# The compression MLP's first product in true fp32 on four column tiles, from raw weights in idle buffers

## The reference, cut to what matters

```python
blk_idx = arange(15)[:, None] * 16 + arange(32)[None, :]       # 15 blocks of 32 tokens, stride 16
def compress(x, w1, w2, pe):                                     # x: (B, 256, 2 heads, 128)
    xb = x[:, blk_idx] + pe[None, None, :, None, :]
    xb = moveaxis(xb, 3, 2).reshape(B, 15, 2, 32 * 128)
    return gelu(xb @ w1) @ w2                                    # w1: (4096, 128), w2: (128, 128)
kc = compress(k_cmp, cmp_w1[0], cmp_w2[0], cmp_pe[0])
vc = compress(v_cmp, cmp_w1[1], cmp_w2[1], cmp_pe[1])
```

## Time and profile before

| | |
|---|---|
| median of 3 runs | 1335.93 us |
| span of the profiled execution | 1336.1 us |
| PE (matmul) busy | 1319.3 us, 99% |
| PEld (weight load) busy | 967.8 us, 72% |
| DVE busy | 581.0 us, 43% |
| ACT busy | 487.0 us, 36% |
| POOL busy | 28.6 us, 2% |
| DMA | 364.96 MB, mean 273 GB/s |

### The profile page before, as it was taken

One profiled execution on the slowest core, in us unless ns is written; L12 is line 12 of the kernel. 1 busy time (PEld: TensorE's weight loads), 2 busy tenths in 40 slices (PEclk: granted clock), 3 DMA queues, 4 the chain that ended last, 5 costly groups with the idle time before them and its releaser, 6 DMA issues.

```text
span 1336.1 us, 17829 instructions
## 1 busy us (share of the span) xinstructions
PE 1319.3 (99%) x7317; PEld 967.8 (72%) x7317; DVE 581.0 (43%) x752; ACT 487.0 (36%) x678; POOL 28.6 (2%) x50
## 2 busy tenths in 40 slices
PE   8999999999999999999999999999999999999898
PEld 8999989998888888888888888854444444534343
DVE  4387444446555545554445555525111121121206
ACT  4454444435465644454333434422121221211212
POOL 1000000400000000000100001000000000000000
PEclk9999999999999999999999999999999999999999
DMA  9767555545545445654556795799999999999996
GB/s 304 259 196 261 178 189 189 189 159 166 173 137 179 155 149 173 192 162 163 183 198 215 265 391 187 254 383 415 422 421 420 422 421 422 421 420 422 421 408 244
DMA packets 122099, 364.96 MB, mean 273 GB/s; under 512 B 11627, under 2 KB 19243, under 8 KB 98486
## 3 DMA queue, kind: packets, MB, share of 16 engines
q1 hardware_dynamic: 115430, 359.06, 72.6%
q10 hardware_dynamic: 6608, 5.02, 1.3%
HBM read 361.96 MB, written 2.10 MB: 272 GB/s over the span
## 4 chain that ended last, share of the span: by engine, by line
PE 93%; DMA 4%; DVE 1%; SPq 1%; ACT 0%; issue 0%; DVEq 0%
PE main L1204 19%; PE main L1206 19%; PE main L1205 19%; PE main L561 16%; PE att L651 7%; PE att L515 5%; DMA mraw<-in_expert_w_down_dram 3%; PE att L1453 1%; DMA raw<-in_w_in_dram 1%; PE main L527 1%; PE main L528 1%; PE att L1436 1%; PE att L1472 1%; PE att L1468 1%; PE att L1423 0%; PE att L622 0%
## 5 line engine op out<-in xcount | busy, mean ns | idle before, releaser
L1870 DVE TENSOR_TENSOR wlo<-raw,whi 128x2048 fp32r<-128x2048 f32 x134 | 308.1, 2299 | 354.1 <-ACT whi L1619 354.1
L1619 ACT ACTIVATE whi<-raw 128x2048 fp32r<-128x2048 f32 x134 | 256.1, 1911 | 413.7 <-PE main L1206 410.7
L561 PE MATMUL main<-mraw,xg 128*64 128x512 f32 x1024 | 225.3, 595 | 0.7 <-DMA mraw<-in_expert_w_up_dram 0.6
L1204 PE MATMUL main<-whi,xhi 128*128 128x512 f32 (+1 forms) x544 | 203.8, 375 | 0.0
L1206 PE MATMUL main<-whi,xlo 128*128 128x512 f32 (+1 forms) x544 | 201.7, 371 | 0.0
L1205 PE MATMUL main<-wlo,xhi 128*128 128x512 f32 (+1 forms) x544 | 201.5, 370 | 0.0
L561 PEld LDWEIGHTS main<-mraw,xg 128*64 128x64 f32 x1024 | 71.9, 137 | 136.9 <-issue 134.9
L1204 PE MATMUL main<-xhi,whi 128*128 128x256 f32 (+1 forms) x560 | 159.5, 285 | 1.6 <-DVE wlo L2002 1.0
L1205 PE MATMUL main<-xlo,whi 128*128 128x256 f32 (+1 forms) x560 | 158.4, 283 | 0.0
L1206 PE MATMUL main<-xhi,wlo 128*128 128x256 f32 (+1 forms) x560 | 158.4, 283 | 0.0
L1206 PEld LDWEIGHTS main<-whi,xlo 128*128 128x128 f32 x544 | 102.5, 188 | 17.7
(11 more groups left out here) (345 smaller groups left out, 1353.8 us busy)
## 6 DMA issues: line engine op xcount, KB each, us to landing
raw<-in_w_in_dram SPq DMA_DIRECT2D x95, 1024.0 KB, 5.0
mraw<-in_expert_w_gate_dram SPq DMA_DIRECT2D x64, 1024.0 KB, 22.6
mraw<-in_expert_w_up_dram SPq DMA_DIRECT2D x64, 1024.0 KB, 23.7
mraw<-in_expert_w_down_dram SPq DMA_DIRECT2D x58, 1024.0 KB, 24.4
raw<-in_w_branch_dram SPq DMA_DIRECT2D x24, 1024.0 KB, 5.0
raw<-in_w_out_dram SPq DMA_DIRECT2D x16, 1024.0 KB, 6.4
mraw<-in_expert_w_down_dram SPq DMA_DIRECT2D x12, 512.0 KB, 8.2
xin<-in_x_dram SPq DMA_DIRECT2D x4, 512.0 KB, 8.1
```

The source lines that it names most:

```text
L561: ins = pe.matmul(main[0][half, w, :], xg[:, k, half], src[:, kk * DE:(kk + 1) * DE], start=(k == 0), stop=(k == KT - 1))
L1204: pe.matmul(o, ah, bh, start=start, stop=False, skip_group_check=skip)
L1619: act.activation(whi[:, u % SPLIT, 0:n], raw[:, slot, 0:n], ACT.Copy).then_inc(hi_done, 1)
L1870: dve.tensor_tensor(wlo[:, u % SPLIT, 0:n], raw[:, slot, 0:n], whi[:, u % SPLIT, 0:n].bitcast(F32), ALU.subtract).then_inc(lo_done, 1)
```

## The change

The four units of `cmp_w1` leave the ring. SyncE loads them unsplit into four buffers that nothing uses yet, each right after the ring's loads of units 9 to 12. The sum of windows and `pe` is written with a stride of 32 in place of 30, the two columns left over are set to zero by VectorE, and its high and low parts are not made. TensorE computes, for each position l, a true fp32 matmul with a stationary 128x32 and a moving 128x128, on column tile l mod 4; tile n gathers the positions with l mod 4 = n. The four partial sums lie in the four groups of 32 partitions. One fp32 matmul for each of keys and values, against `pick` (four identities of 32, made by GpSimd), adds them and transposes. All later units of the ring are four numbers lower, and the work hung on them moves with them. Some semaphores are merged.

```diff
-        w1u = len(units)
-        for j in range(2):
-            for q in range(2):
-                src = A["cmp_w1"][0, j, q * 2048:(q + 1) * 2048, :].rearrange("(l p) m -> p l m", p=P)
-                units.append((src, 16, P))
-        HALVED = [1, *range(w1u, w1u + 5)]
+        HALVED = [1]
-        xpk = at("xpk", R + 4096, [P, XP])
+        xpk, xpv = at("xpk", R + 4096, [P, CMP, CT]), at("xpv", O1, [P, CMP, CT])
+        w1 = [at(f"w1_{n}", o, [P, 16, P]) for n, o in enumerate((made["qaT"], made["qbT"], O2 + 8192, O1 + 4096))]
@@ SyncE, after load(u, ...)
+                if SLC0 <= u < SLC0 + 4:
+                    n = u - SLC0
+                    rows = A["cmp_w1"][0, n // 2, n % 2 * 2048:(n % 2 + 1) * 2048, :]
+                    sp.dma_start(w1[n][:], rows.rearrange("(l p) m -> p l m", p=P)).then_inc(w1_in[n // 2], 16)
@@ GpSimd, at the start
+            ch.link(pool.memset(pick[:], 0.0))
+            for n in range(P // CT):
+                ins = pool.affine_select(out=pick[:], in_=pick[:], compare_op=ALU.not_equal, fill=1.0, base=-CT * n,
+                                         pattern=[[-1, CT]], channel_multiplier=1)
...
@@ TensorE
-            for j, (xh, xl) in enumerate(((xpkh, xpkl), (xpvh, xpvl))):
...
-                        ins = mm3(att[0:LB * KV * NC, 3 - 2 * j, :], xh[:, cols], xl[:, cols],
...
+            for j, x_ in enumerate((xpk, xpv)):
+                pe.wait_ge(xp_sum, j + 1)
+                pe.wait_ge(w1_in[j], 32)
+                for l in range(CMP):
+                    n = l % (P // CT)
+                    ins = pe.matmul(att[n * CT:(n + 1) * CT, 3 - 2 * j, 0:P], x_[:, l, :], w1[2 * j + l // 16][:, l % 16, :],
+                                    start=(l < P // CT), stop=(l >= CMP - P // CT), skip_group_check=True)
+            ins.then_inc(xp_ps, 1)
@@ TensorE, compress2, after the first unit of win
-                        for l in range(LB):
-                            ins = pe.matmul(att[:, 3, j * 32:j * 32 + n], cs[0:LB * n, j, l * P:(l + 1) * P],
...
+                        ins = pe.matmul(att[:, 3, j * CT:(j + 1) * CT], cs[:, j, :], pick[:], start=(j == 0), stop=True,
+                                        skip_group_check=True)
@@ ScalarE, extra(u)
-                if u == 12:
-                    for j, (a, b) in enumerate(((xpk, xpkh), (xpv, xpvh))):
...
-                if u == w1u + 5:
-                    act.wait_ge(unit_used, w1u + 4)
+                if u == last("slc") + 2:
+                    act.wait_ge(xp_ps, 1)
-                if u == w1u + 7:
+                if u == last("slc") + 4:
@@ VectorE, extra(u)
                 if u == 11:
+                    for dst in (xpk, xpv):
+                        ins = dve.memset(dst[:, :, KV * NC:], 0.0)
+                    link(ins)
...
-                if u == 13:
-                    for j, (a, b, c) in enumerate(((xpk, xpkh, xpkl), (xpv, xpvh, xpvl))):
...
-                if 19 <= u < 23:
+                if 15 <= u < 19:
                     top_rounds(2)
```

More of the change, by code:

```diff
@@ L55 @@
 C_QB, C_CKV, C_QI, C_KI, C_UV, C_GM = 2584, 3608, 3864, 4120, 4188, 6236
-LB = 4
 CW, CG = 16, 32
+CT = 32
 NKI = ID + IH
@@ L197, in build @@
         kcT, vcT = at("kcT", R, [P, KV, S]), at("vcT", R + 2048, [P, KV, S])
-        XP = CMP * KV * NC
-        xpk = at("xpk", R + 4096, [P, XP])
[L200 to L204, removed]
+        xpk, xpv = at("xpk", R + 4096, [P, CMP, CT]), at("xpv", O1, [P, CMP, CT])
+        w1 = [at(f"w1_{n}", o, [P, 16, P]) for n, o in enumerate((made["qaT"], made["qbT"], O2 + 8192, O1 + 4096))]
         ws = at("ws", O1 + 12288, [P, GG, P])
@@ L221, in build @@
         smT = at("smT", made["pT"] + 7168, [P, S])
-        cs = at("cs", made["wuk"], [P, 2, LB * P])
+        cs = at("cs", made["wuk"], [P, 2, P])
+        pick = at("pick", made["wuk"] + 2048, [P, CT])
         score = at("score", made["sig"], [P, 3 * P])
@@ L319, in build @@
         part_in = [sem(f"part_in{k}") for k in range(4)]
-        gn_in, pe_in, pe_ps, pe_out, w2_in, kvg_in, late_in = sems("gn_in pe_in pe_ps pe_out w2_in kvg_in late_in")
+        gn_in, pe_in, pe_ps, pe_out, early_in, late_in = sems("gn_in pe_in pe_ps pe_out early_in late_in")
         ki_ps, ki_out, ix_ps, ix_sum, ix_mask = sems("ki_ps ki_out ix_ps ix_sum ix_mask")
         c_ssq, c_var, c_std, c_norm, c_ps, c_out = sems("c_ssq c_var c_std c_norm c_ps c_out")
-        xp_sum, xp_hi, xp_lo, cs_out, g1_ps, g1_out, cc_ps, cc_out = sems("xp_sum xp_hi xp_lo cs_out g1_ps g1_out cc_ps cc_out")
-        ws_in, ws_ps, ws_out, ws_ok, gsig = sems("ws_in ws_ps ws_out ws_ok gsig")
+        xp_sum, xp_ps, cs_out, g1_ps, g1_out, cc_ps, cc_out = sems("xp_sum xp_ps cs_out g1_ps g1_out cc_ps cc_out")
+        w1_in = [sem(f"w1_in{j}") for j in range(2)]
+        ws_ps, ws_out, ws_ok, gsig = sems("ws_ps ws_out ws_ok gsig")
         v_var, v_std, v_nrm, v_ok, mix_ps, mix_u, oc_hi = sems("v_var v_std v_nrm v_ok mix_ps mix_u oc_hi")
@@ L1034, in build @@
         block = ctx.enter_context(nc.Block())
-        N_CONST = 1 + 2 * T + HEADS + 1 + 5
+        N_CONST = 1 + 2 * T + HEADS + 1 + 5 + 1
+        SLC0 = chunks["slc"][1]
         @block.sync
@@ L1141, in _ @@
                 pool.memset(blank, 0.0).then_inc(consts, 1)
+            ch.link(pool.memset(pick[:], 0.0))
+            for n in range(P // CT):
+                ins = pool.affine_select(out=pick[:], in_=pick[:], compare_op=ALU.not_equal, fill=1.0, base=-CT * n,
+                                         pattern=[[-1, CT]], channel_multiplier=1)
+                if n < P // CT - 1:
+                    ch.link(ins)
+            ins.then_inc(consts, 1)
             pool.wait_ge(ix_sum, 1)
@@ L1366, in compress2 @@
                     pe.wait_ge(cs_out, 1)
-                    n = KV * NC
+                    pe.wait_ge(consts, N_CONST)
                     for j in range(2):
-                        for l in range(LB):
-                            ins = pe.matmul(att[:, 3, j * 32:j * 32 + n], cs[0:LB * n, j, l * P:(l + 1) * P],
-                                            ident[0:LB * n, l * n:(l + 1) * n], start=(j == 0 and l == 0),
-                                            stop=(l == LB - 1), skip_group_check=True)
+                        ins = pe.matmul(att[:, 3, j * CT:(j + 1) * CT], cs[:, j, :], pick[:], start=(j == 0), stop=True,
+                                        skip_group_check=True)
                     ins.then_inc(g1_ps, 1)
@@ L1375, in compress2 @@
                     pe.wait_ge(g1_out, 1)
-                    pe.wait_ge(w2_in, 16)
+                    pe.wait_ge(early_in, 48)
                     pe.matmul(att[:, 3, 0:KV * NC], w2[:, 0, :], g1[:], start=True, stop=True)
@@ L1381, in compress2 @@
                 if u == last("win"):
-                    pe.wait_ge(ws_in, 16)
+                    pe.wait_ge(early_in, 48)
                     for g in range(GG):
@@ L1687, in extra @@
                     act.activation(rstd[:], ssq[:], ACT.Sqrt).then_inc(c_std, 1)
-                if u == 12:
-                    for j, (a, b) in enumerate(((xpk, xpkh), (xpv, xpvh))):
-                        act.wait_ge(xp_sum, j + 1)
-                        act.activation(b[:], a[:], ACT.Copy).then_inc(xp_hi, 1)
                 if u == last("slc") + 3:
@@ L1694, in extra @@
                     act.activation(cT[:].rearrange("p c s -> p (c s)"), att[:, 2, :], ACT.Copy).then_inc(c_out, 1)
-                if u == w1u + 5:
-                    act.wait_ge(unit_used, w1u + 4)
+                if u == last("slc") + 2:
+                    act.wait_ge(xp_ps, 1)
                     for j in range(2):
-                        ins = act.activation(cs[0:LB * KV * NC, j, :], att[0:LB * KV * NC, 3 - 2 * j, :], ACT.Copy)
+                        ins = act.activation(cs[:, j, :], att[:, 3 - 2 * j, 0:P], ACT.Copy)
                     ins.then_inc(cs_out, 1)
-                if u == w1u + 7:
+                if u == last("slc") + 4:
                     act.wait_ge(g1_ps, 1)
@@ L1760, in _ @@
                 if u == 1:
-                    act.dma_start(w2[:], A["cmp_w2"][0].rearrange("a m d -> m a d")).then_inc(w2_in, 16)
-                    act.dma_start(kvg[:], A["kv_norm_g"].to_broadcast([P, LAT])).then_inc(kvg_in, 16)
-                    act.dma_start(ws[:], A["gmlp_w_s"][0].rearrange("g t s -> t g s")).then_inc(ws_in, 16)
+                    act.dma_start(w2[:], A["cmp_w2"][0].rearrange("a m d -> m a d")).then_inc(early_in, 16)
+                    act.dma_start(kvg[:], A["kv_norm_g"].to_broadcast([P, LAT])).then_inc(early_in, 16)
+                    act.dma_start(ws[:], A["gmlp_w_s"][0].rearrange("g t s -> t g s")).then_inc(early_in, 16)
                 if u in after:
@@ L1932, in extra @@
                     link(dve.reciprocal(rstd[:], rstd[:]))
-                    dve.wait_ge(kvg_in, 16)
+                    dve.wait_ge(early_in, 48)
                     for t in range(T):
@@ L1944, in extra @@
```

(10 more changed lines are left out.)

## The result

The changed kernel took 1328.62 us (median of 4 runs, 1328.30 to 1330.33) where the kernel before took 1335.88 (4 runs in all): 7.3 us faster, ratio 0.9946, interval 0.9935 to 0.9958. A repeat with more runs gave 1327.04 against 1335.71, ratio 0.9937 (0.9924 to 0.9951). The forecast was 1327.6, 8.3 us faster, with a range of 1326.8 to 1331.2.

A forecast was written before the change was run, and what follows sets the result against it. PE, busy 99% of the span, was taken to bound the kernel. Product -7.4, gathering -1.25 and VectorE +0.3 gave -8.3 us, from the median 1335.93 to 1327.6 us; whole range 1326.8 to 1331.2.

The forecast's parts named there:

- The product: First product on PE: 32 waves of four records at 0.110 us plus 0.32, so 11.26 to 3.9 us, saving 7.4.
- the edges: Entering and leaving the tiled product on PE: 0.32 us once, taken from the router's step.
- The Trainium skill's rule: Weight loads overlap running matmuls only where the row group differs; column tiles share it, so the product's loads would be exposed.
- rival 1: First product: each wave takes its stream, then its load, 0.218 us; product 7.3 us, kernel 1331.0 us; chance 0.12.
- The factor of 3.07: First product: the skill's speedup for four row tiles, not 4; by it the product takes 5.2 us, the kernel 1328.9.
- The gathering: Gathering matmuls on PE: four records in place of 16, 1.78 to 0.53 us, saving 1.25 (1.1 to 1.4).
- VectorE before unit 12: Two zero fills at VectorE's u = 11, where it has no slack, cost PE 0.3 us (0.1 to 0.6).
- The DMAs: Four cmp_w1 loads in the full queue, 3.9 us per MB, cost nothing: cover of 11 us or more each.
- The sum: Whole kernel: -7.4 - 1.25 + 0.3 = -8.3 us, from the median 1335.93 to 1327.6 us.
- The later stages: After the changed place, the rest of the trace shifts by one amount, the experts' DMA-bound stage starting earlier too.
- rival 2: First product: no side-by-side running, loads exposed, 0.134 us a record; product 17.5 us, kernel 1341.2 us; chance 0.04.
- rival 3: DMA queue: each cmp_w1 load costs 9.8 us, PE waits 6.2 and 0.6 at units 12 and 13; 1334.4 us; chance 0.04.

The follow-up runs named there:

- tile runs: Changed kernel with the first product's 64 matmuls on one column tile, or on two, in place of four: 1338.73 us and 1330.96 us.
- early loads: Changed kernel with the four cmp_w1 loads issued together right after the ring's load of unit 6: 1332.53 us.

## Why the prediction was right, point by point

- **The product**, forecast 11.26 to 3.9: it takes 3.63 plus 0.2 of edges, 3.83. The wave of 0.110, from the experts' two tiles, is met to 0.001; the edges, from the router's step, were put 0.1 too high. Shown by one, two and four tiles.
- **The Trainium skill's rule** on row groups ("TensorE: Matmul & The Clock Gate", Part 3) would have made each wave wait for its loads. The waves are 0.111 us with loads recorded at 110 ns, so the rule does not hold for these column tiles, and rival 1, which I gave 0.12, is refuted. The trace of before already spoke against it in the ordinary stream, where the loads below, on all rows, stand between matmuls that start every 0.12 us:
```profile
L1204 PEld LDWEIGHTS main<-xhi,whi x560: 157/192/192, 8.3 to 312.8; 128*128 128x128 f32 x182, 128*92 128x92 f32 x5
```
The factor of 3.07, which the same part gives for four row tiles, is not what four column tiles give here: 14.09 / 3.63 = 3.9.
- **The gathering**, forecast -1.25: measured 1.78 to 0.44, -1.34.
- **VectorE before unit 12**, forecast +0.3: the gap grew by 0.27. That VectorE's order makes it is shown by moving the fills and the second sum.
- **The DMAs**, forecast hidden: they were. A load of `cmp_w1` cost some 3.5 us of the full queue, not 3.9; unit 12 landed at 62.4 (forecast by 63), unit 13 at 68.5 (73), the last weights at 65.8 (67). That the clock adds to a stall I had not weighed.
- **The sum**, forecast 8.3: TensorE gained 8.5 at the changed place in both profiles of the changed kernel. That the first comparison shows just 8.3 at the router is luck, because the start of that execution had gone 0.2 slower.
- **The later stages**, forecast "one amount": true up to the router, and then each profile goes its own way. The first comparison gave 7.3, the repeat 8.7, and the intervals of both hold 8.5. Profiles of one kernel differ by 1.25 us at the fillers, with the clock, and by 1.3 in the experts' stage. I had counted the profile of before as a usual execution, which it was not; the forecast was counted from the median and did not suffer by it. My 2.7 us for what can be told was generous; but 1 us is not told by 4 runs.
- **Rivals 2 and 3** are refuted: rival 2 by the waves of the changed kernel and by the tile runs, rival 3 by the splits that PE still released and by the early loads.

## What to carry to other kernels

Price tiled fp32 matmuls by the wave: the records that go to different column tiles cost together what one costs alone, down to 128 moving columns and 32 stationary ones. Where TensorE is the bound, look at every instruction that is added to another engine in the stretch ahead: here 0.22 us of fills on an engine without slack became a gap of 0.27 more on TensorE. And before comparing two kernels at 1 us, compare two profiles of one kernel; here they differed by 3.3.

## What the runs showed of the hardware that I had not expected

- A stall of 3.75 us on TensorE was followed, 1.2 us after it resumed, by 3.5 us at the 1.2 GHz level, which cost 1.5 us more.
- The same fall came in three profiles and not in the five others at the router's fillers (32 records in 5.45 us, or in 3.82), with the same instructions ahead of it and no wait of TensorE over 0.4 us there.
- In a full queue a load with 512-byte rows cost 3.6 us per MB when four stood in a row, and 3.4 to 3.5 when each stood between loads with 2 KB rows, which cost 2.7 to 3.1.
- Four fp32 records over 32 or 64 rows cost 0.75 us between full matmuls, and 0.44 over 128 rows.
